# Fillers of constants at TensorE's waits, and native products inside three early pairs of each feed-forward

## What the kernel computes

```python
h = x
for i in range(2):                                   # first block
    proj = rmsnorm(h, norm_g[i]) @ w_in[i]
    # 4 heads of a gated linear recurrence (chunked scan), 8 heads of sparse attention
    # (compressed keys, selected blocks, a window), gates
    h = h + concat(y_hg, y_nsa) @ w_out[i]
    h = h + sigmoid(rmsnorm(h, ple_norm_g[i]) @ w_pg[i]) * (p[i] @ w_pp[i])
x = h
for i in range(2):                                   # second block
    x = layer_norm(a*x + 0.5*swiglu_ffn(x, ffn_w_in[i,0], ffn_w_out[i,0]))   # feed-forward
    x = layer_norm(a*x + (diff_attention(x) if i == 0 else pool_mixer(x)))
    x = layer_norm(a*x + memory_cross_attention(x, mem))
    x = layer_norm(a*x + 0.5*swiglu_ffn(x, ffn_w_in[i,1], ffn_w_out[i,1]))   # feed-forward
return x
```

## Time and profile before

| what | value |
|---|---|
| median of 3 runs | 3259.86 us |
| the three runs | 3245.55, 3259.86, 3285.77 us |
| the profiled execution, its own time | 3264.66 us |
| its span, first to last instruction | 3262.8 us |
| TensorE busy | 3075.0 us, 94% of the span |
| mean granted TensorE clock | 0.970 |
| VectorE, ScalarE, GpSimd busy | 35%, 34%, 41% |

### The profile page before, as it was taken

The page is one execution under the profiler, slowest core; times in us unless marked ns, Lnnn a source line. Parts: engine busy times, 40 slices in busy tenths (PEclk is TensorE's granted clock), DMA queues, the critical chain, the costliest instruction groups (busy, mean ns, idle before and its releaser), DMA issues.

```text
span 3262.8 us, 58662 instructions
## 1 busy us (share of the span) xinstructions
PE 3075.0 (94%) x24228; PEld 2822.0 (86%) x24228; DVE 1140.7 (35%) x1896; ACT 1121.7 (34%) x1893; POOL 1352.5 (41%) x648
## 2 busy tenths in 40 slices
PE   7998998999899999999899999999999987999998
PEld 7986588987488999888489799998999977789997
DVE  1535642534743211242761531104111083531103
ACT  4333633233633222222633332223222153332222
POOL 5433045433144444444046254544444444254443
PEclk9998999999999999999989999999999998999999
DMA  5211023212012232222014122232222232122221
GB/s 195 67 65 52 1 78 110 72 46 72 7 65 92 90 102 98 94 71 91 1 53 154 39 84 96 96 103 71 95 95 98 92 104 71 59 80 94 90 97 58
DMA packets 72059, 261.19 MB, mean 80 GB/s; under 512 B 8016, under 2 KB 8656, under 8 KB 70896
## 3 DMA queue, kind: packets, MB, share of 16 engines
q1 hardware_dynamic: 69728, 249.77, 23.2%
q10 hardware_dynamic: 2192, 9.44, 0.8%
HBM read 257.09 MB, written 2.10 MB: 79 GB/s over the span
## 4 chain that ended last, share of the span: by engine, by line
PE 87%; DVE 9%; ACT 3%; issue 1%; DMA 0%; POOL 0%; ACTq 0%; DVEq 0%; POOLq 0%
PE bank L522 25%; PE bank L504 16%; PE bank L506 16%; PE bank L508 16%; PE bank L663 1%; PE bank L836 1%; PE bank L868 1%; PE bank L852 1%; PE bank L1077 1%; DVE small L2155 1%; PE bank L1068 1%; PE bank L714 1%; DVE padded L2245 1%; DVE tb L1787 1%; PE bank L906 1%
## 5 line engine op out<-in xcount | busy, mean ns | idle before, releaser
L390 POOL TENSOR_TENSOR wl<-raw,wh 128x1024 fp32r<-128x1024 f32 x464 | 1152.6, 2498 | 1795.9 <-ACT wh L1160 1795.8
L1160 ACT CAST wh<-raw 128x1024 fp32r<-128x1024 f32 x464 | 472.1, 1048 | 1024.0 <-PE bank L508 803.7
L504 PE MATMUL bank<-xh,wh 128*128 128x256 f32 x3168 | 641.7, 284 | 0.0
L506 PE MATMUL bank<-xl,wh 128*128 128x256 f32 x3168 | 625.7, 279 | 0.0
L508 PE MATMUL bank<-xh,wl 128*128 128x256 f32 x3168 | 625.2, 279 | 0.0
L504 PEld LDWEIGHTS bank<-xh,wh 128*128 128x128 f32 x3168 | 484.5, 189 | 19.5 <-issue 18.1
L508 PEld LDWEIGHTS bank<-xh,wl 128*128 128x128 f32 x3168 | 484.2, 190 | 0.0
L506 PEld LDWEIGHTS bank<-xl,wh 128*128 128x128 f32 x3168 | 483.6, 190 | 0.0
L522 PE MATMUL bank<-xh,wh 128*128 128x256 f32 x1952 | 395.4, 285 | 54.1 <-ACT xh L1222 37.6
L522 PE MATMUL bank<-xh,wl 128*128 128x256 f32 x1952 | 392.6, 283 | 0.0
L522 PEld LDWEIGHTS bank<-xh,wh 128*128 128x128 f32 x1952 | 305.5, 194 | 65.2 <-issue 64.5
(11 more groups left out here) (335 smaller groups left out, 3792.9 us busy)
## 6 DMA issues: line engine op xcount, KB each, us to landing
raw<-in_slabs SPq DMA_DIRECT2D x464, 512.0 KB, 3.3
h<-in_x_t SPq DMA_DIRECT2D x8, 256.0 KB, 5.5
w1v<-in_w ACTq DMA_DIRECT2D x2, 1024.0 KB, 4.8
side<-in_pp_w ACTq DMA_DIRECT2D x2, 1024.0 KB, 5.2
out<-h SPq DMA_DIRECT2D x8, 256.0 KB, 2.0
side<-in_w SPq DMA_DIRECT2D x1, 1024.0 KB, 12.6
vt<-in_p_t ACTq DMA_DIRECT2D x2, 512.0 KB, 6.6
side<-in_w ACTq DMA_DIRECT2D x1, 1024.0 KB, 7.0
```

The source lines that it names most:

```text
L390: nc.gpsimd.tensor_tensor(wl[:, n % RING, :], raw[:, n % RING, :], wh[:, n % RING, :], A.subtract).then_inc(w_low, 1)
L504: nc.tensor.matmul(dst[:, c], high_l, high_r[:, c], start=first and n == 0, stop=False)
L506: nc.tensor.matmul(dst[:, c], high_l, low_r[:, c], start=False, stop=False)
L1160: nc.scalar.copy(wh[:, slot, :], raw[:, slot, :]).then_inc(w_high, 1)
```

## The change

Two helpers are added to TensorE's part. `keep_clock(times, b)` issues native products of 384 columns, constants by constants, into a PSUM bank that nothing reads then. `break_pace()` issues one of 512 columns. The fillers stand: at the very start (4); behind the last statistics product of five layer norms that follow a feed-forward or an output projection (8 each); behind that of the two root-mean-square norms ahead of `front` (7 each) and of the layer norm behind the pooling mixer (8); ahead of the scan in layer 1 (6); in `group_stats` (5); in `nsa`, per layer, 4 ahead of the score step of unit 1 and 3 behind it; behind `xa` in each layer (3). That is 97 fillers. The layer norm ahead of the pooling mixer and the last one have none, nor have the root-mean-square norms ahead of `pg`. `ffn_in` calls `products` three times in place of once: the second, third and fourth pair of 22 get a `break_pace()` ahead of their step k = 4, twelve in all; no weight, order or wait of the pairs is changed.

```diff
@@ -509,6 +509,15 @@
+            def keep_clock(times, b):
+
+                for _ in range(times):
+                    nc.tensor.matmul(bank[b][:, 0:3 * P], mean_m, cst[:, 0:3 * P], start=True, stop=True)
+
+            def break_pace():
+
+                nc.tensor.matmul(bank[7][:], mean_m, cst[:, 0:T], start=True, stop=True)
+
@@ -546,7 +555,8 @@
-            def products(st, slab, ticket, step, pairs, split_base, act_h=xh, act_l=xl, w=T, resumed=False):
+            def products(st, slab, ticket, step, pairs, split_base, act_h=xh, act_l=xl, w=T, resumed=False,
+                         broken=()):
@@ -566,6 +576,8 @@
                         two_steps = (high_in, low_in) if split_base is not None and j == 0 else ()
+                        if j in broken:
+                            two_steps = (lambda k: break_pace() if k == 4 else None,)
                         pair(slab + 2 * j, j, act_h, act_l, w, *two_steps).then_inc(prod, 1)
@@ -617,6 +629,8 @@
                     nc.tensor.matmul(b_sq, mean_m, sq[:, 1, :], start=False, stop=True).then_inc(S["stat"], 1)
+                    if st["kind"] == "ln" and (st["layer"], st["which"]) not in ((1, 0), (1, 3)):
+                        keep_clock(8, 7)
                     return
@@ -625,6 +639,7 @@
                 last.then_inc(S["stat"], 1)
+                keep_clock(8 if st["kind"] == "ln" else 7, 7)
@@ -725,6 +740,8 @@
+                if st["layer"]:
+                    keep_clock(6, 7)
                 for lv in range(LEVELS):
@@ -798,6 +815,7 @@
+                keep_clock(5, 7)
                 pe.wait_ge(S["grs"], st["grs"] + 1)
@@ -877,9 +895,12 @@
                         pe.wait_ge(S["ev_v"], st["ev_v"])
+                        keep_clock(4, 4)
                     more = u + 1 < UNITS
                     if more:
                         score_step(u + 1, 0)
+                    if u == 0:
+                        keep_clock(3, 5)
@@ -926,7 +947,9 @@
             def ffn_in(st):
-                products(st, st["slab"], st["took"], st["prod"], NF, st["xl"] - KC)
+                products(st, st["slab"], st["took"], st["prod"], 2, st["xl"] - KC, broken=(1,))
+                products(st, st["slab"] + 4, st["took"] + 2, st["prod"] + 2, 2, None, resumed=True, broken=(0, 1))
+                products(st, st["slab"] + 8, st["took"] + 4, st["prod"] + 4, NF - 4, None, resumed=True)
@@ -1090,6 +1113,7 @@
                 values_of(3)
+                keep_clock(3, 4)
@@ -1131,6 +1155,7 @@
             pe.wait_ge(consts_made, 3)
+            keep_clock(4, 7)
```

## The result

| | before | after |
|---|---|---|
| median of 18 runs each | 3247.2 us | 3287.6 us |
| lowest to highest | 3238.8 to 3285.8 | 3281.4 to 3297.2 |
| profiled execution | 3264.7 | 3287.6 |
| mean granted TensorE clock | 0.970 | 0.985 |
| TensorE busy | 94% | 96% |

The ratio is 1.0106, with a 95% interval from 1.0087 to 1.0124: the changed kernel is 1% slower. I had forecast 3248 us, a small gain, with a range to 3270 us. The result also shows that the profiled execution of before, with two slow feed-forwards, was not a typical one: its 3264.7 us lie 17 us above the median of 18, about one slow feed-forward more.

A forecast was written before the change was run, and what follows sets the result against it. TensorE, busy for 94% of the span, was taken as the bound, through its pace and clock. From the profiled 3264.7 us, +10.4 natives, -12.2 fillers and -13.6 pace gave 3249, put at 3248 us; range 3230 to 3270.

The forecast's parts named there:

- the term for the pace: Four feed-forwards: natives in pairs 2, 3 and 4 would leave fewer stages at the slow pace, -13.6 us.
- one slow in place of two: Feed-forwards: of the profiled execution's two slow stages one would stay slow; chance of one left 0.35.
- Natives, +10.4 us: Twelve native products in `ffn_in`, on TensorE's path with nothing hiding them: 0.87 us each, +10.4 us.
- Fillers, -12.2 us: 97 native products at waits keep TensorE's clock up: gains of 3.4, 3.4, 3.2 and 2.2 us, -12.2 us together.
- the layer norm shown: Layer norm ahead of products: eight fillers gain 0.6 us of the 1.5 that the clock costs.
- the scan's first steps in layer 1: Six fillers ahead of the scan: first scan step to third chunk step from 7.62 to 5.5 us, gain 2.2.
- The start: Fillers before the first TensorE work: bounds -1 to +1 us, taken as 0.
- `nsa`: Sparse attention, fillers around unit 1's score step: bounds -2 to +3 us per layer, taken as 0.
- 3 chances in 4: Feed-forwards: chance that a stage ends at the fast pace, weighing `da_project`'s five fast stretches of six more.
- The third rival: Feed-forwards: single natives leave the slow pace as a rule, all four end slow, 3290 us; three or four slow, chance 0.1.
- the split into three calls of `products`: `ffn_in`: same waits in the same order, three loops in place of one, taken at nothing.
- the 109 ns: Split products of 256 columns: the skill page's single warm gap, with no second pace; cited as speaking against the edit.

The follow-up runs named there:

- the twelve doubles: The changed kernel with each of the 12 interruptions made two native products of 512 columns in a row in place of one: 3246.8 us, ratio 0.9969 to before.

## Why the prediction was wrong

The natives and the fillers held; the term for the pace had the wrong sign. The base, 3264.7 us, fits an execution with two slow feed-forwards, as I had said. But the median of 18 is 3247.2, which looks like one slow stage, so "one slow in place of two" would have been hardly a gain over the usual execution even if it had come.

- *Natives, +10.4 us: right.* In the changed kernel the two neighbouring natives at 1028.01 and 1040.18 us are 12.17 us apart, 0.86 more than a slow pair of 11.31; I had 0.87 each. The timeline of TensorE of the changed kernel:

```profile
1028.01 1.02 PE L519 MATMUL bank<-cst 128*128 128x512 f32 x2
...
1040.18 1.02 PE L519 MATMUL bank<-cst 128*128 128x512 f32 x2
```

- *Fillers, -12.2 us: right in the sum*, 12.6 with all stages slow and 12.5 with all fast, as far as separate sets of runs can tell. Of its parts the layer norm shown gave 0.5 for 0.6; the scan's first steps in layer 1 take 605.70 - 600.17 = 5.53 us for the forecast 5.5. The start gave 2.7 us where I had counted 1.5: TensorE's first split product comes at 21.04 us, where it came at 22.39, and the first 192 take 22.83 us in place of 24.22. For `nsa` I had 0, and the traces give at most 1.4 per layer.
- *The pace of the feed-forwards, -13.6 us: this step failed.* It read: "From `da_project`, whose pairs are the same work with natives at the same k, five of six stretches are fast"; and from that, 3 chances in 4. The cases were not alike. `rotate_pair` issues two natives, `break_pace` one. I treated the pace behind an interruption as drawn by lot, with the number of natives without meaning. The runs showed that it isn't drawn: one native of 512 columns made a fast stream slow in 12 cases of 12, four of them in the changed kernel; two of 512 left a fast one fast in 14 of 14, in the feed-forwards of all traces. Doubling the natives, with nothing else changed, took 41 us off the time. Four slow stages in place of two are +27 us, and the whole difference to the forecast is 27 + 13.6 = 40.6; measured, 3287.6 - 3248 = 39.6.
- The third rival, "the natives break fast streams", named this mechanism and gave 3290 us; even its condition was right, a single native that leaves the slow pace as a rule where two don't. I gave it one chance in ten. It was never asked what differs between the stretches of `da_project`. Ahead of the natives of the slow one at 1413 us TensorE had waited 2.32 us for VectorE; ahead of those of the five stretches at the fast pace it had not:

```profile
1408.40 3.65 PE L972 MATMUL bank<-tb,cst 128*128 128x512 f32 x4 [2.32 <-DVE dq L2140]
```

  That wait doesn't decide either, for in the changed kernel the same natives come behind a wait of 2.0 us and the stretch behind them is fast; but it makes this row a poor witness for natives alone. The slow 28 us behind 1505 us are another matter. There two natives stand in `token_major`, a loop that orders its products otherwise, and in all 14 traces the stream is fast ahead of them and slow behind. So the number of natives alone is no rule either. And the range ended at 3270, below a mechanism that I had priced.
- I had also read the split into three calls of `products` as issuing the same waits in the same order. It does not, as the page after shows; the kernel with the split alone took 3255.8 us, so this error cost nothing that shows.
- The Trainium skill's page "TensorE: Matmul & The Clock Gate" gives, in "Back-to-back issue gap", N/2.4 GHz + 2.5 ns as the warm gap of an isolated product, from which I had the 109 ns. It says there, as I did not, that in a stream of weight loads and products both set the spacing; it has stream figures for 128 and 512 columns, none for 256, and no second pace. The traces show two: 444 and 427 products in 50 us at a granted clock of 1.00. In the section on the HAM clock gate it puts the ramp penalty below 1% of a typical span. The fillers' 12.5 us are 0.4%, which is in line, but they are only what the fillers gave back: the mean clock after is still 0.985.

The measured times fit together with the same few terms. From the kernel with natives of 128 columns (3227.6 us) to the changed one it is 60.0 us: 12 x (0.86 - 0.22) = 7.7 for the wider natives, and 52.3 for four slow stages, if every execution of the first has four feed-forwards at the fast pace, 13.1 each, where the rates gave 13 (14.2 less the early pairs). To the twelve doubles it is 12 x (1.72 - 0.22) = 18.0, measured 19.2.

## What to carry to other kernels

Read the rate of a long stream from starts or counts at a like clock, in several places and executions, before any of its time is put down to work: here the same products took 113.3 or 117.8 ns each, for whole stages, and the variation of the kernel's time between runs fits steps of one slow stage. If an interruption is to steer such a stream, measure the very instruction, its width and its number, behind a slow and a fast entry; a cousin of it in the same trace can do the opposite. Fillers at a wait pay where the clock falls and TensorE comes next; behind a norm whose chunks come one by one, ask first what supplies them.

## What the runs showed of the hardware

- TensorE has two paces for a stream of products of 256 columns at full granted clock, 113.3 and 117.8 ns from start to start (444 and 427 in 50 us), and keeps either through more than 2200 products. A slow stream can turn fast within a dozen products behind an interruption. Twice a slow pair outside the feed-forwards turned fast in its middle, with no native and no idle time of TensorE there (the kernel with the three calls alone, at 1773 us, and the one without the fillers of `nsa`). From fast to slow it went only behind an interruption or a wait instruction.
- At k = 4 of a feed-forward's pair, two natives of 512, 384 or 256 columns or one of 128 left a fast stream fast (51 of 51), and one, three or four of 512, one of 384 or 256 and two of 128 made it slow (19 of 19, four of these at other k). Behind a slow stream the same interruption did different things at different places. One of 128 ended fast in nine stages of nine, in three kernels; two of these came in slow. What in the machine decides stays open; no experiment here reached it.
- A kernel whose pace is steered varies less: the changed one lies within 15.8 us in 18 runs, the one before within 47.0.
